# Output projections of a pooling and a latent-attention block: ordinary products in pairs replaced by seven block products

## The reference

```python
def pool_layer(x, norm_g, w_in, w_group, scale, w_out):
    uz = rmsnorm(x, norm_g) @ w_in            # u, z: 2048 wide each
    pooled = windowed means of u - u          # 4 groups of 512
    y = (pooled @ w_group, by group) * scale * silu(z)
    return x + y @ w_out                      # 512 x 2048 @ 2048 x 1024

def mla_layer(x, ...):                        # 16 heads of 128
    y = causal_mla_attention(...) * silu(z)   # 512 x 2048
    return x + y @ w_out                      # 512 x 2048 @ 2048 x 1024
```

## Time and profile before

| what | us |
|---|---|
| median of 3 executions | 1304.98 (1304.48 to 1305.07) |
| the profiled execution, device time | 1304.71 |
| its span in the profile | 1303.0 |
| TensorE (PE) busy | 1293.0 |
| its weight loads (PEld), overlapping | 1093.0 |
| VectorE (DVE) busy | 826.7 |
| ScalarE (ACT) busy | 586.1 |
| GpSimd (POOL) busy | 454.0 |

### The profile page before, as it was taken

How to read it: one execution, slowest core, us unless ns; L and a number is a source line. 1 busy time by engine, 2 the same in 40 slices (tenths; PEclk the granted TensorE clock), 3 DMA queues, 4 the chain that set the end, 5 groups by cost and what they waited for, 6 DMA issues and landing times.

```text
span 1303.0 us, 17714 instructions
## 1 busy us (share of the span) xinstructions
PE 1293.0 (99%) x6826; PEld 1093.0 (84%) x6826; DVE 826.7 (63%) x1200; ACT 586.1 (45%) x976; POOL 454.0 (35%) x208
## 2 busy tenths in 40 slices
PE   9999999999999999999999999999999999999998
PEld 7888888888778888888888787898879999998886
DVE  7999728233292466665434575567989999985442
ACT  5224323222333466656633345568464444443223
POOL 2444544444444442452544342323430000015441
PEclk9999999999999999999999999999999999999999
DMA  4333423333723422226143345433323223323331
GB/s 163 97 97 105 128 83 97 97 97 97 274 81 97 129 65 82 82 64 212 49 161 97 114 146 153 125 104 124 96 67 130 98 99 113 114 83 112 113 95 67
DMA packets 47870, 143.60 MB, mean 110 GB/s; under 512 B 6032, under 2 KB 6032, under 8 KB 47024
## 3 DMA queue, kind: packets, MB, share of 16 engines
q1 hardware_dynamic: 43984, 129.88, 32.0%
q10 hardware_dynamic: 3808, 12.64, 2.7%
HBM read 121.46 MB, written 10.49 MB: 101 GB/s over the span
## 4 chain that ended last, share of the span: by engine, by line
PE 95%; ACT 1%; DVE 1%; issue 1%; DMA 1%; POOL 0%; SPq 0%; POOLq 0%; ACTq 0%
PE bank L1867 30%; PE bank L1869 30%; PE bank L1868 30%; PE bank L2039 2%; PE bank L2028 1%; PE bank L2029 1%; DMA x<-x_in 1%; PE bank L1891 0%; POOL w_lo L624 0%; DVE zv L1600 0%; ACT f_prob_t L871 0%; PE bank L2354 0%; PE bank L2184 0%; PE bank L2185 0%; ACT pool_xg L718 0%
## 5 line engine op out<-in xcount | busy, mean ns | idle before, releaser
L624 POOL TENSOR_TENSOR w_lo<-raw,w_hi 128x1024 fp32r<-128x1024 f32 (+1 forms) x146 | 359.7, 2467 | 543.9 <-ACT w_hi L692 543.7
L692 ACT ACTIVATE w_hi<-raw 128x1024 fp32r<-128x1024 f32 x149 | 156.2, 1054 | 233.7 <-PE bank L1869 183.3
L669 POOL TENSOR_TENSOR w_lo<-raw,w_hi 128x1024 fp32r<-128x1024 f32 x22 | 53.5, 2437 | 263.3 <-DVE w_lo L1724 204.7
L1867 PE MATMUL bank<-y_hi,w_hi 128*128 128x512 f32 x256 | 101.5, 396 | 0.0
L1868 PE MATMUL bank<-y_lo,w_hi 128*128 128x512 f32 x256 | 101.3, 396 | 0.0
L1869 PE MATMUL bank<-y_hi,w_lo 128*128 128x512 f32 x256 | 101.2, 395 | 0.0
L1867 PE MATMUL bank<-pool_xg,w_hi 128*128 128x512 f32 x248 | 98.5, 397 | 0.2 <-POOL w_lo L624 0.2
L1868 PE MATMUL bank<-pool_xg,w_hi 128*128 128x512 f32 x248 | 98.1, 396 | 0.0
L1869 PE MATMUL bank<-pool_xg,w_lo 128*128 128x512 f32 x248 | 98.1, 395 | 0.0
L1867 PE MATMUL bank<-right,w_hi 128*128 128x256 f32 x336 | 94.4, 281 | 0.0
L1869 PE MATMUL bank<-right,w_lo 128*128 128x256 f32 x336 | 94.1, 280 | 0.0
(11 more groups left out here) (410 smaller groups left out, 3549.0 us busy)
## 6 DMA issues: line engine op xcount, KB each, us to landing
raw<-stream SPq DMA_DIRECT2D x187, 512.0 KB, 3.6
raw_x<-stream SPq DMA_DIRECT2D x18, 512.0 KB, 4.7
spill<-x ACTq DMA_DIRECT2D x2, 2048.0 KB, 6.8
xg_spill<-mla_xg ACTq DMA_DIRECT2D x2, 2048.0 KB, 11.9
rope_q<-turned_hl SPq DMA_DIRECT2D x64, 64.0 KB, 2.5
zx<-xg_spill SPq DMA_DIRECT2D x2, 1536.0 KB, 8.6
stacked<-fq SPq DMA_DIRECT2D x24, 128.0 KB
stacked<-fk SPq DMA_DIRECT2D x24, 128.0 KB
```

The costliest lines, as they stand in the source:

```text
L624: pool.tensor_tensor(w_lo[:, j % RING, 0:width], raw[:, j % RAW, 0:width], plain(w_hi[:, j % RING, 0:width]), ALU.subtract).then_inc(tile_ ...
L669: pool.tensor_tensor(w_lo[:, s, 0:D], raw[:, d % RAW, 0:D], plain(w_hi[:, s, 0:D]), ALU.subtract).then_inc(tile_lo, 1)
L692: act.activation(w_hi[:, t % RING, 0:width], raw[:, t % RAW, 0:width], ACT.Copy).then_inc(tile_hi, 1)
L1867: pe.matmul(target, a_hi, b_hi, start=start, stop=False)
```

## The change

In both projections the second half of K is no longer done chunk by chunk for all chunks. All tiles are reordered (`OUT_TILES`). The first half of K stays ordinary for every chunk ("first" tiles). The second half of K of output chunks 0 and 1, 2 and 3, and in pooling 4 and 5, is done by seven block products for a pair, after Strassen and Winograd: the 1,024 by 512 by 256 product is cut in two along tokens, K and outputs, and has two tiles ("direct", "crossed"). Each of the seven products is 4 K-chunks by three matmuls of 256 columns: 84 matmuls in place of 48 of 512. They go to four banks (`CELL_BANKS`, c, a, b, d), half of it each.

The right side needs four differences t1 to t4 of blocks of z, their high parts (ScalarE) and low parts, and the low parts of the blocks themselves: `right_operands` on VectorE, once per projection, with the first pair's weight sums in its middle. Low parts 8 to 15 of y are no longer made one by one. The left side needs, for each pair, three sums of raw weights (`weight_sums`, one of 1,024 and two of 512 elements), cast by ScalarE (`weight_casts`), and their low parts by VectorE (`weight_lows`, two of 1,024). ScalarE copies the pair's first cell (`copy_first`); VectorE's `combine` puts the cells together into x. SyncE's loads of tiles into `raw` wait also for the sums that read the slot. GpSimd's work is unchanged, and there are as many tiles as before. The buffers of the squares move to other addresses.

At the decay heads: the low parts of query and key chunk 1 (and ScalarE's cast of the key chunk) move behind the first transposed low parts of head 0; at head 7 half of the weighing moves ahead of the last mixing.

```diff
+OUT_TILES = {"pool_out": (*(("first", m) for m in range(5)), ("direct", 0), ("crossed", 0), ("first", 5), ("direct", 1),
+    ("crossed", 1), ("first", 6), ("direct", 2), ("crossed", 2), ("second", 6), ("first", 7), ("second", 7)),
+             "mla_out": (*(("first", m) for m in range(6)), ("direct", 0), ("crossed", 0), ("first", 6), ("direct", 1),
+    ("crossed", 1), ("second", 4), ("second", 5), ("second", 6), ("first", 7), ("second", 7))}
+OUT_PAIRS = {"pool_out": 3, "mla_out": 2}
+CHUNK_BANK = {"pool_out": (0, 1, 2, 3, 4, 1, 6, 3), "mla_out": (0, 1, 2, 3, 4, 1, 6, 0)}
+CELL_BANKS = {"pool_out": ((5, 6, 7, 0), (2, 3, 4, 5), (0, 1, 7, 2)), "mla_out": ((5, 6, 7, 0), (2, 3, 7, 5))}
+TAKEN_BEFORE = {"pool_out": (1, 5, 6), "mla_out": (1, 4)}
+COMBINED_BEFORE = {"pool_out": ({}, {"s3": 2}, {"a11": 2, "s3": 4}), "mla_out": ({}, {"a12": 2})}
+OUT_SIGNALS, OUT_CUTS = 5, 7
+OUT_SUMS = 3
...
-for turn, j in sweep(sp, TILE["heads"]):
+def out_loads(stage):
+    for j in range(7, PC - 1):
+        kind, i = OUT_TILES[stage][j - RAW]
+        if kind in ("direct", "crossed"):
+            sp.wait_ge(out_summed, OUT_SUMMED + OUT_SUMS * (out_pair(stage, i) + 1))
+        load(0, TILE[stage] + j)
...
-    for k in range(first, PC):
+def out_stage(stage, n, gained, square, first=0):
+    def weight_casts(i):
+        p = out_pair(stage, i)
+        act.wait_ge(out_summed, OUT_SUMMED + OUT_SUMS * (p + 1))
+        act.wait_ge(out_product_done, PRODUCT_DONE + OUT_SIGNALS * p)
+        for r in range(2):
+            act.activation(out_w_hi[:, r, :], out_sums[:, r, :], ACT.Copy).then_inc(out_cast, 1)
+    def copy_first(i):
+        if i:
+            act.wait_ge(n.x_ready, 2 * i)
+        p = out_pair(stage, i)
+        act.wait_ge(out_product_done, PRODUCT_DONE + OUT_SIGNALS * p + 1)
+        act.activation(out_parts[:, 0, :], cells(stage, i)[0][:, TOKENS[0]], ACT.Copy, scale=-1.0).then_inc(first_copied, 1)
+    if first == 0:
+        split_tile(stage, 0, 0)
+    done = 4 * (stage == "mla_out")
+    for i, t in enumerate(T_ORDER):
+        act.wait_ge(t_summed, T_SUMMED + done + i + 1)
+        act.activation(out_t_hi[:, t], out_t[:, t], ACT.Copy).then_inc(t_cast, 1)
+    pooling = stage == "pool_out"
+    copies, casts = ((5, 8, 11), (3, 7, 10)) if pooling else ((6, 9), (4, 8))
+    squares = {7: (0, 1), 10: (2, 3)} if pooling else {8: (0, 1), 11: (2, 3)}
+    last_chunks = {13: (4, 5), 14: (6,)} if pooling else {12: (4,), 13: (5,), 14: (6,)}
+    for k in range(1, PC):
         split_tile(stage, 0, k)
-        if k >= 3 and k % 2:
-            norm_chunk((k - 3) // 2)
...
+    if k in copies:
+        copy_first(copies.index(k))
+    if k in casts:
+        weight_casts(casts.index(k))
+    if k == (13 if pooling else 11):
+        act.wait_ge(out_product_done, PRODUCT_DONE + OUT_SIGNALS * out_pair(stage, OUT_PAIRS[stage]))
+        for c in range(4):
+            gained(c)
+    for c in squares.get(k, ()):
+        square(c)
+    for c in last_chunks.get(k, ()):
+        gained(c)
+        square(c)
+gained(DC - 1)
+square(DC - 1)
...
+t1, t2, t3, t4 = (out_t[:, i] for i in range(4))
+dve.wait_ge(ready, PC)
+dve.tensor_tensor(t1, b12, b11, ALU.subtract).then_inc(t_summed, 1)
+dve.wait_ge(t_summed, T_SUMMED + done + 1)
+dve.tensor_tensor(t2, b22, t1, ALU.subtract).then_inc(t_summed, 1)
+dve.wait_ge(t_summed, T_SUMMED + done + 2)
+dve.tensor_tensor(t4, b21, t2, ALU.subtract).then_inc(t_summed, 1)
+dve.tensor_tensor(t3, b12, b22, ALU.subtract).then_inc(t_summed, 1)
+dve.wait_ge(t_summed, T_SUMMED + done + 4)
+dve.wait_ge(y_hi_done, y_count)
+def y_block_low(r, half):
+    dve.tensor_tensor(block_of(y_lo, r, half), block_of(z, r, half), plain(block_of(y_hi, r, half)),
+                      ALU.subtract).then_inc(t_cut, 1)
+def t_block_low(i):
+    dve.wait_ge(t_cast, T_CAST + done + T_ORDER.index(i) + 1)
+    dve.tensor_tensor(out_t_lo[:, i], out_t[:, i], plain(out_t_hi[:, i]), ALU.subtract).then_inc(t_cut, 1)
+y_block_low(2, 0)
+t_block_low(3)
+dve.tensor_tensor(y_lo[:, 12:16, :], z[:, 12:16, :], plain(y_hi[:, 12:16, :]), ALU.subtract).then_inc(t_cut, 1)
+t_block_low(1)
+weight_sums(stage, 0)
+t_block_low(2)
+t_block_low(0)
+y_block_low(2, 1)
...
+    dve.wait_ge(tile_loaded[u % RAW], 16 * (u // RAW + 1))
+dve.wait_ge(out_cut, OUT_CUT + 2 * p)
+direct, crossed = raw[:, t % RAW, 0:D], raw[:, (t + 1) % RAW, 0:D]
+dve.tensor_tensor(halves(out_sums[:, 1, :]), halves(direct), both(crossed[:, HALF_D:D]), ALU.add).then_inc(out_summed, 1)
+dve.wait_ge(out_summed, OUT_SUMMED + OUT_SUMS * p + 1)
+dve.tensor_tensor(out_sums[:, 0, HALF_D:D], out_sums[:, 1, HALF_D:D], direct[:, 0:HALF_D], ALU.add).then_inc(out_summed, 1)
+dve.wait_ge(out_summed, OUT_SUMMED + OUT_SUMS * p + 2)
+dve.tensor_tensor(out_sums[:, 0, 0:HALF_D], out_sums[:, 0, HALF_D:D], crossed[:, 0:HALF_D], ALU.add).then_inc(out_summed, 1)
...
+def take(m):
+    dve.wait_ge(tile_used, TILE[stage] + out_at(stage, "first", m) + 1)
+    dve.tensor_tensor(x[:, m, :], out_bank(stage, CHUNK_BANK[stage][m])[:], x[:, m, :], ALU.add).then_inc(bank_taken, 1)
...
+def combine(i):
+    p, m = out_pair(stage, i), 2 * i
+    c, a, b, d = cells(stage, i)
+    u4, u2, u3 = (out_parts[:, j, :] for j in range(1, 4))
+    product = PRODUCT_DONE + OUT_SIGNALS * p
+    dve.wait_ge(bank_taken, BANK_TAKEN + 2 * out_pair(stage, 0) + m + 2)
+    dve.wait_ge(first_copied, FIRST_COPIED + p + 1)
+    dve.wait_ge(out_product_done, product + 2)
+    settle(dve.tensor_tensor(u2, c[:, TOKENS[1]], out_parts[:, 0, :], ALU.add))
+    dve.wait_ge(out_product_done, product + 3)
+    settle(dve.tensor_tensor(x[:, m, :], b[:], x[:, m, :], ALU.add))
+    dve.wait_ge(out_product_done, product + 4)
+    settle(dve.tensor_tensor(u3, d[:, TOKENS[0]], u2, ALU.add))
+    settle(dve.tensor_tensor(halves(x[:, m + 1, :]), halves(x[:, m + 1, :]), both(u3), ALU.add))
+    dve.wait_ge(out_product_done, product + 5)
+    settle(dve.tensor_tensor(u4, a[:, TOKENS[1]], u2, ALU.add))
+    dve.tensor_tensor(halves(x[:, m, :]), halves(x[:, m, :]), out_parts[:, 0:2, :], ALU.subtract).then_inc(n.x_ready, 1)
...
+    for m in range(3):
+        take(m)
+    weight_lows(0)
+    take(3)
+    if stage == "pool_out":
+        take(4)
+    weight_sums(stage, 1)
+    combine(0)
+    weight_lows(1)
+    total(0)
+    total(1)
+    if stage == "pool_out":
+        take(5)
+        weight_sums(stage, 2)
+        combine(1)
+        weight_lows(2)
+        total(2)
+        total(3)
+        combine(2)
+        dve.wait_ge(n.x_ready, 6)
+        for k in range(6):
+            low(k)
+        take_last(6)
+        total(4)
+        total(5)
+        low(6)
+        total(6)
+    else:
+        combine(1)
+        dve.wait_ge(n.x_ready, 4)
+        for k in range(4):
+            low(k)
+        total(2)
+        total(3)
+        for k in range(4, 7):
+            take_last(k)
+            low(k)
+            total(k)
+    take_last(7)
+    low(7)
+    total(7)
...
-    if c:
+    if 0 < c <= HALF_K:
         y_low(c - 1)
-y_low(PC - 1)
+right_operands("pool_out", y_ready, PC)
...
-    if h == HEADS - 1:
-        product_low(range(8, 14))
...
-product_low(range(14, PC))
+right_operands("mla_out", mla.out, 2 * PC)
...
-qk_low(2)
-qk_low(3)
 for h in range(FOX_HEADS):
     transposed_low(fox, h, f_prob_t_hi, f_prob_t_lo, (0, 1))
+    if h == 0:
+        qk_low(2)
+        qk_low(3)
...
+def out_product(stage, n, first=0):
+    taken = BANK_TAKEN + 2 * out_pair(stage, 0)
+    for j, (kind, i) in enumerate(OUT_TILES[stage]):
+        if (kind, i) == ("first", 4) and stage == "pool_out":
+            pe.wait_ge(y_ready, PC)
+        if kind == "direct":
+            out_seven(stage, n, i)
+        elif kind != "crossed" and j >= first:
+            if (kind, i) == ("first", 5):
+                pe.wait_ge(bank_taken, taken + 2)
+            elif (kind, i) == ("first", 6):
+                pe.wait_ge(n.x_ready, 2)
+            elif (kind, i) == ("first", 7):
+                pe.wait_ge(n.x_ready, 4)
+            elif kind == "second":
+                pe.wait_ge(t_cut, T_CUT + OUT_CUTS * (1 + (stage == "mla_out")))
+            out_tile(stage, j, range(8))
...
+pe.wait_ge(bank_taken, BANK_TAKEN + 2 * out_pair(stage, 0) + TAKEN_BEFORE[stage][i])
+wait_combined("a11")
+wait_tile(0, t)
+pe.wait_ge(t_cut, cuts + 1)
+half_k_product(c, 0, direct, 0, y_block(2, 0), out_product_done)
+pe.wait_ge(t_cut, cuts + 2)
+half_k_product(a, 0, direct, 1, t_block(3), tile_used)
+wait_combined("a12")
+wait_tile(0, t + 1)
+pe.wait_ge(t_cut, cuts + 3)
+half_k_product(b, 0, crossed, 0, y_block(3, 0), tile_used)
+pe.wait_ge(out_cut, OUT_CUT + 2 * p + 1)
+pe.wait_ge(t_cut, cuts + 4)
+pe.wait_ge(first_copied, FIRST_COPIED + p + 1)
+half_k_product(c, 1, sums_42, 1, t_block(1), out_product_done)
+half_k_product(b, 1, sums_42, 0, y_block(3, 1), out_product_done)
+wait_combined("s3")
+pe.wait_ge(out_cut, OUT_CUT + 2 * p + 2)
+pe.wait_ge(t_cut, cuts + 5)
```

(43 more changed lines are left out.)

129 lines of the change are left out of this document (91 added, 38 removed).

## The result

The changed kernel takes 1313.03 us (median of 6 runs, 1311.62 to 1313.73) against 1304.93 before (6 runs, 1304.48 to 1305.13): ratio 1.0061, 95% interval 1.0051 to 1.0071. It is slower, as forecast, but by 8.1 us instead of 4.4, and half a microsecond outside the stated range. The profiled execution is the fastest of the six: 1311.62 us, span 1309.9, so 6.9 above the one of before in both.

What follows compares the result with a forecast made beforehand. TensorE, busy 99% at full clock, was taken as the bound. 1304.7 + 5.4 (MLA) + 0.5 (pooling) - 1.3 (decay heads) = 1309.3, kept as 1309.4 us; range 1299.5 to 1312.5.

Steps and rivals of the forecast that it cites:

- The saving, 1.24 us a pair: TensorE, both projections: 84 short matmuls (9.98 us) replace 48 long ones (11.21 us); five pairs save 6.2 us.
- GpSimd's low parts stop VectorE for some 2.3 us each: Both projections: each GpSimd weight low part, once per 5.6 us tile, stops VectorE's chain about 2.3 us.
- MLA, 5.9 for take 1: MLA, tile 5: TensorE waits 5.9 us until VectorE has added bank 1 to x; bounds 1.2 and 8.2.
- MLA, 2.0 for the combination: MLA, behind the first pair: first-half chunk 6 waits 2.0 us for the pair to be combined; bounds 1.7 and 4.3.
- One stop more: MLA combination, upper bound: one further GpSimd stop of VectorE makes the wait 4.3 us.
- Any wait put in front of a matmul is paid in full.: TensorE, whole kernel: busy 99% at clock 1.00, no slack, so each added wait costs its length.
- Pooling, waits of 0.5, 1.8 and 1.9: Pooling: 0.5 us before the sixth product, then 1.8 and 1.9 for ScalarE's first-cell copies of pairs two and three; net +0.5.
- Decay heads, -1.3: First head about -0.85 us, last head -0.45, as waits vanish or shrink; together -1.3, bounds 0 and -2.
- (1): Both projections: port costs little, stops fall into gaps; MLA waits 1.2 + 2.0, pooling keeps 3.7; 1300.4 us, chance 0.26.
- (2): Only MLA is late, +5.4; pooling's copies come in time; 1305.1 us, no change, chance 0.16.
- (3): Loads land later when a finished sum releases two at once, about 4 us more; 1313 us, chance 0.07.
- (4): Projections: weight loads pace the short matmuls at 188 ns each, five pairs add 29 us; 1338 us, chance 0.01.

Runs made afterwards that it cites:

- best2: Changed kernel with the edits of take_early, bank and casts together, plus ScalarE's casts and copy of MLA's second pair moved earlier as in pooling: 1297.41 us.
- no_low2: Changed kernel with GpSimd's low-part subtraction cut to 16 of 1,024 columns for all 32 weight tiles of both projections, a test with incomplete result: 1299.88 us.
- take_early: Changed kernel with VectorE taking banks 0 and 1 in MLA before the first weight sums instead of behind them and three low parts: 1307.05 us.
- the repeat: The changed kernel measured once more with no edit: 1313.19 us.
- filled: Changed kernel with 20 and 12 unused matmuls of 512 columns ahead of MLA's waits for take 1 and for the combined pair: 1308.68 us.
- casts: Changed kernel with ScalarE, in pooling, casting sums of pairs 1 and 2 before splitting tiles 10 and 13, and copying first cells earlier: 1310.14 us.
- fox: Kernel before the change with only the reorderings around the first and last decay heads: 1303.83 us.
- sums_last: Changed kernel with MLA's first weight sums placed behind all low parts of the right side instead of between them: 1311.17 us.
- bank: Changed kernel with MLA's first half of chunk 6 in chunk 2's bank instead of pair 0's second cell, second pair's cells fitted: 1307.98 us.

## Why the prediction was right or wrong

- **The saving, 1.24 us a pair.** Right. Pooling without waits is 3.7 shorter (three pairs, 3.7); MLA in best2 2.1 (two, 2.5).
- **GpSimd's low parts stop VectorE for some 2.3 us each.** Right, a little too high: the operations of 3.42, 4.50, 2.77 and 2.27 us were stopped for 2.2, 2.2, 2.1 and 1.6. It decides the case, as no_low2's 13 us show. The Trainium skill's rule on who keeps the port (SBUF — State Buffer, Who interferes with whom) fits the rows: GpSimd's low part began at 659.60, 0.2 us ahead of VectorE's long operation, which then took 4.50 = 2.2 + 2.3 (2.31 without the stop, in no_low2). How a nearer tie falls was not tried by itself.
- **MLA, 5.9 for take 1.** Near: 5.3 named, 5.45 start to start. Take 1 was at 27.9 where 28.3 was said, each turn of the chain was where the forecast had it, and take_early removed the whole wait.
- **MLA, 2.0 for the combination.** Mis-sized: 3.4. "One stop more" stood as the upper bound, 4.3, and one stop came; without stops it is 1.9 (no_low2).
- **"Any wait put in front of a matmul is paid in full."** This is the step that failed. The two long waits were paid with 1.5 us on top each, and in the repeat's profile with 1 more, since the clock fell to 0.5. It was no term of the sum and of no rival, so the range ended too low; a row that showed a fall was not in the trace of before, whose clock was 1.00 throughout. With it, 5.45 + 3.4 + 3.0 to 4.0 - 2.5 = +9.4 to +10.4 for MLA instead of +5.4. filled shows the term by itself: 4.5 us.
- **Pooling, waits of 0.5, 1.8 and 1.9.** The two on the copy were there, with 1.78 and 1.46 start to start; the first was not. Hence -0.6 instead of +0.5. The cause is the one that was named, ScalarE in order behind a split that has to wait, and casts shows it; but only the second pair's split waited for a load, the third's for TensorE.
- **Decay heads, -1.3.** Measured -1.0 by the medians of fox, at the edge of noise; -1.3 by its marks, of which 0.2 returns.
- **Rivals.** (1) would have needed the stops to fall into gaps; they did not. (2) had pooling right in sign but not MLA. (3) named nearly the measured time, 1313, by loads that land later; that is a coincidence: MLA's sums began at 18.5 (18.7 forecast) and pooling's tile 10 was split at 44.2 (load due at 44.7), and the time came from the clock and the combination. (4) is out by best2.

The sum, term by term, for the first profile: 1309.3 forecast, + 4.0 in MLA (clock 3.0, combination 1.4, take 1 -0.4), - 1.1 in pooling, - 0.1 at the heads and - 0.5 in stages that the edit does not touch makes 1311.6, as measured; the median is 1.4 above it. Pooling's error thus hid part of MLA's: without it the miss would have been about 1 us larger. The missing term is positive wherever the forecast has a long wait, so the upper end of the range should have had it too.

## What to carry to other kernels

Where a kernel's TensorE never stands, price a new wait twice: its length, and the slow stretch behind it, if it is long. Here stands of 1.2 to 2.1 us cost only themselves; behind those of 2.3 to 5.3 the clock was at 0.5 for 7 matmuls of 512 columns or more. Work that goes to an engine "half idle" must be laid against the engine that shares its port, operation by operation; and a bank or a copy that the critical engine waits for belongs ahead of whatever stands for a load. Reorderings of that kind, without touching the arithmetic, turned 8 us more into 7.7 less.

## What was not expected of the hardware

The clock fell already behind a stand of 2.3 us (sums_last, granted clock 0.66 on average from 699 to 704), though not behind one of 2.1 in pooling (filled). It does not always fall during the stand: behind the second stand of the repeat the first three matmuls lasted 0.50, 0.39 and 0.39 us, as at full speed, before those of 0.63 came. How long it then stays low differs between executions of the same kernel: 8 matmuls behind the first stand in one, 13 in the other, which is 1.0 of the 1.9 us between the two profiles; behind the same stand it was 11 in casts and 14 in bank. What sets this length no run here shows. An interval that is all "busy" can thus hold 1.5 us of loss; the granted clock and the counts of matmuls in a window show it, the busy time does not.
